# VectorE cuts part of the low halves of the weight panels behind each norm

## The chip, the cores and the metric

The kernel runs on one core of a Trainium2 chip. The metric is device time in microseconds of one execution. The engines are TensorE (PE; its weight loads are shown as PEld), VectorE (DVE), ScalarE (ACT), GpSimd (POOL) and SyncE (SP), which issues the loads of weights.

## What is computed

The reference takes 512 tokens of width 1024 through two blocks of layers, all in float32. Ten stages follow one another. Each ends in a layer norm:

```python
x = layer_norm(DEEPNORM_ALPHA * x + mix, g, b)
# stages: even mixer, cross attention to a memory, swiglu, odd mixer, cross attention, swiglu,
#         hgrn2 + forgetting attention, swiglu, rg_lru + stick-breaking attention, swiglu
def memory_cross_attention(x, mem, wq, wkv, wo):   # mem: 256 tokens
    q = x @ wq;  k, v = split(mem @ wkv)
    return softmax(q k^T) v @ wo
```

Most of the work is products of the 512 (or, for the memory, 256) tokens with weights of width 1024 or 2816.

## The kernel before, in words

**Products.** Float32 values are split in two: a high part, rounded to the type that TensorE multiplies (float32r), and a low part, the difference. `product` (lines 482 to 486) makes each product of three matmuls: high by high, high by low, low by high. So each weight has to be there as a high and a low part.

**Panels.** The weights come in 230 panels of 1 MB (128 partitions by 2048 columns), in the order in which TensorE uses them. Three buffers hold raw panels (`raw`), three hold high parts (`whi`); the low part `wlo` overwrites the raw panel in place. SyncE issues panel n when TensorE is done with panel n-3. The high part is a copy into float32r, in two halves of 1024 columns, by GpSimd (line 2353) or, for the panels in `cut_panels`, by ScalarE (`act_cut`, line 613). The low part is raw minus high, on GpSimd in four quarters of 512 columns (line 2361), one panel after the other. The one exception is the very first panel: VectorE makes its second half (line 2399). TensorE waits in `next_panel` (line 477) for the count of panels that GpSimd has finished:

```python
                for q in range(4 if n else 2):
                    cs = slice(512 * q, 512 * q + 512)
                    ...
                    m = pool.tensor_tensor(wlo[b][:, cs], raw[b][:, cs], whi[b][:, cs].bitcast(F32), ALU.subtract)
                m.then_inc(panel_split, 1)
```

**The end of a stage.** `pe_block_out` multiplies by the down projection (4 or 11 panels). The last three panels are used tile by tile of 128 tokens, so that tiles 0 and 1 are finished early. `dve_block_out` normalises each tile on VectorE: `centre` (lines 721 to 726) adds the product to x and takes off the mean, ScalarE takes the deviation (lines 689, 692), `finish` (lines 732, 733) writes the normalised row. The order on VectorE is centre 0 and 1, finish 0 and 1, the low parts of the turned tiles 0 and 1 (`dve_turn`, line 593), centre 2 and 3, finish 2 and 3. TensorE turns the tiles (`pe_turn`, line 573): tiles 0 and 1 between the last products, tiles 2 and 3 inside the head of the next stage.

**The head of the next stage.** Behind seven of the nine inner norms the next stage uses its first two panels on half of the tokens first (`pe_split`), needing only tiles 0 and 1; tiles 2 and 3 are turned in the middle of the second panel. Behind the other two (before the cross attention stages) come eight panels of `mem_wkv`, called M1 to M8 below, which need no tokens of x: M1 to M3, the turns of tiles 2 and 3, then M4 to M8, and then four panels of the query projection. M1 to M4 use 256-column products, M5 to M8 half as many of 512 columns. Of the panels behind a norm, counted from its last one, ScalarE makes the high parts of 1 and 2 and, before cross attention, of 5 to 8 too.

**Norm rows.** At the start of each stage ScalarE's queue issues two loads (`ln_gb`), 0.5 MB each, which spread the norm's gain and bias over the partitions.

Of the kernel before, what the change touches and what calls it, by code (L numbers as in the profile page):

```python
# [39 lines left out]
NB = 3  # L40
# [13 lines left out]
def build(nc, a, out, stages):  # L54
    with ExitStack() as ctx:
# [220 lines left out]
        panel_hi = sem("panel_hi")  # L276
        panel_hi_act = sem("panel_hi_act")
        panel_split = sem("panel_split")
        first_lo = sem("first_lo")
        panel_used = sem("panel_used")  # L280
        phase = {e: sem(f"phase_{e}") for e in ("pe", "act", "dve")}
        par_loaded = sem("par_loaded")
# [190 lines left out]
        def next_panel(pe, n=1):  # L473

            first = used[0]
            used[0] += n
            pe.wait_ge(panel_split, used[0])
            if first == 0:
                pe.wait_ge(first_lo, 1)
            return [(whi[k % NB], wlo[k % NB]) for k in range(first, first + n)]  # L480

        def product(pe, o, lhs, rhs, start, stop):
# [102 lines left out]
        def dve_turn(dve, dst_hi, dst_lo, k0, blocks, bank, t, gain=None):  # L585
# [3 lines left out]
            for b in range(0, blocks, 4):  # L589
# [4 lines left out]
                else:  # L594
# [9 lines left out]
                               for k in ((0, 1, 2, 5, 6, 7, 8) if program[i + 1:] and program[i + 1][0][0] == "cross"  # L604
                                         else (0, 1, 2)) if n + k < len(panels)]

        def act_cut(act, n):
            assert n in cut_panels
            b = n % NB
            act.wait_ge(panel_loaded[b], 16 * (n // NB + 1))  # L610
            for q in range(2):
                cs = slice(1024 * q, 1024 * q + 1024)
                act.activation(whi[b][:, cs], raw[b][:, cs], ACT.Copy).then_inc(panel_hi_act, 1)  # L613
# [95 lines left out]
        def dve_block_out(dve, step, head, ln_loaded):  # L709
            base = n_ln["dve"]  # L710
            n_ln["dve"] += NT
            dve.wait_ge(*ln_loaded)

            def two_banks(t):
                return PS[:, 2 * t:2 * t + 2, :].rearrange("p a b -> p (a b)")

            def centre(t):

                xt = x_row[:, t, :]
                dve.wait_ge(y_ready, base + t + 1)  # L720
                step(dve.scalar_tensor_tensor(out=xt, in0=xt, scalar=ALPHA, in1=two_banks(t), op0=ALU.mult, op1=ALU.add,  # L721
                                              accum_out=zsum[:, t:t + 1]))
                dve.tensor_scalar(nmean[:, t:t + 1], zsum[:, t:t + 1], -1.0 / D, None, ALU.mult).then_inc(mean_ready, 1)
                dve.wait_ge(mean_ready, base + t + 1)

                step(dve.scalar_tensor_tensor(out=two_banks(t), in0=xt, scalar=nmean[:, t:t + 1], in1=ln_gb[:, 0, :],
                                              op0=ALU.add, op1=ALU.mult))

            def finish(t):

                dve.wait_ge(std_ready, base + t + 1)
                step(dve.reciprocal(rstd[:, t:t + 1], std[:, t:t + 1]))
                dve.scalar_tensor_tensor(out=x_row[:, t, :], in0=two_banks(t), scalar=rstd[:, t:t + 1], in1=ln_gb[:, 1, :],
                                         op0=ALU.mult, op1=ALU.add).then_inc(row_ready, 1)

            centre(0)
            centre(1)
            finish(0)
            finish(1)
            if head:  # L740
                dve_turn(dve, xT_hi, xT_lo, 0, KD, 0, 0)
                dve_turn(dve, xT_hi, xT_lo, 0, KD, 2, 1)
            centre(2)
            if not head:
                finish(2)
            centre(3)
            if head:
                finish(2)
            finish(3)
            if head:  # L750
                head(dve, lambda: (dve_turn(dve, xT_hi, xT_lo, 0, KD, 4, 2), dve_turn(dve, xT_hi, xT_lo, 0, KD, 6, 3)))
# [150 lines left out]
        def stage_cross(st, jobs):  # L902
# [51 lines left out]
            def act(act, step):  # L954
# [11 lines left out]
                act_units(act, A, lambda u: softmax_exp(act, A, u, PS[:, A.ps(u), 0:MEM], 1.0, MEM, A.p(u)))  # L966
                act_rows(act, 0, KD)

            def dve(dve, step):

                def stat(u):
                    dve.wait_ge(s_ready, A.u0 + u + 1)
# [12 lines left out]
            def pe(pe):  # L985
# [15 lines left out]
                def values(u, k):  # L1001
# [3 lines left out]
                pe_rows(pe, c_row, KD, lambda t: A.g0 + 2 * t + 2)  # L1005
            return {"act_load": act_load, "act": act, "dve": dve, "pe": pe,
                    "memory": {"pe": memory_pe, "act": memory_act, "dve": memory_dve},
                    "head": {"pe": head_pe, "act": head_act, "dve": lambda dve, turns: turns()}}

        def stage_ffn(st, jobs):  # L1010
            n0 = counts.get("ffn_tiles", 0)
# [1331 lines left out]
        def _(pool):  # L2343
            shares = {pool_at[i]: c["pool"] for i, c in enumerate(code) if "pool" in c}
            for n in range(len(panels)):
# [6 lines left out]
                    cs = slice(1024 * q, 1024 * q + 1024)  # L2352
                    pool.tensor_scalar(whi[b][:, cs], raw[b][:, cs], 1.0, 1.0, ALU.mult, ALU.mult).then_inc(panel_hi, 1)  # L2353

                for q in range(4 if n else 2):
                    cs = slice(512 * q, 512 * q + 512)
                    if q % 2 == 0 and by_act:
                        pool.wait_ge(panel_hi_act, 2 * cut_panels.index(n) + q // 2 + 1)
                    elif q % 2 == 0:
                        pool.wait_ge(panel_hi, 2 * (n - sum(k < n for k in cut_panels)) + q // 2 + 1)  # L2360
                    m = pool.tensor_tensor(wlo[b][:, cs], raw[b][:, cs], whi[b][:, cs].bitcast(F32), ALU.subtract)  # L2361
# [30 lines left out]
        def _(dve):  # L2392
# [2 lines left out]
            dve.memset(one_col[:, :], 1.0)  # L2395
            dve.wait_ge(par_loaded, 16)
            dve_turn(dve, xT_hi, xT_lo, 0, KD, 0, 0)
            dve.wait_ge(panel_hi_act, 2)
            dve.tensor_tensor(wlo[0][:, 1024:2048], raw[0][:, 1024:2048], whi[0][:, 1024:2048].bitcast(F32), ALU.subtract)\
                .then_inc(first_lo, 1)  # L2400
            dve_turn(dve, xT_hi, xT_lo, 0, KD, 2, 1)
            code[0]["head"]["dve"](dve, lambda: [dve_turn(dve, xT_hi, xT_lo, 0, KD, 2 * t, t) for t in (2, 3)])
            for i, c in enumerate(code):
                c["dve"](dve, step)
                nxt = code[i + 1] if i + 1 < len(code) else None
                if nxt and "memory" in nxt:
# [146 lines left out]
```

## Time and profile before

| what | value |
|---|---|
| median of 3 runs | 3006.47 us (3005.61 to 3013.05) |
| the profiled execution | 3002.93 us |
| its span, first to last instruction | 3001.1 us |
| mean granted clock of TensorE | 0.992 of full speed |
| GpSimd, low parts of panels (line 2361) | 918 quarters, mean 1337 ns |
| GpSimd, high parts (line 2353) | 384 halves, mean 1105 ns |
| ScalarE, high parts (line 613) | 76 halves, mean 1054 ns |
| a panel's load, issue to landing, median | 5.0 to 5.2 us |

A row of the page's groups names the line, the engine, the operation, its output and inputs, the shape, the count, then busy time in us and the mean of one in ns, and last the idle time of the engine before it with what ended it. In a timeline a row is start, duration, engine, line, operation, tiles, shape and count, and in brackets the idle time before. In the chain of waits a row is start, duration and what ran. Durations on GpSimd are rough, so spacings from start to start are used where they are there.

### The profile page before, as it was taken

How to read it: one execution, taken by the hardware profiler on the slowest of the kernel's cores; microseconds unless marked ns; L12 is line 12 of the kernel's file. 1: busy time of each engine (PE TensorE's matmuls, PEld its weight loads, DVE VectorE, ACT ScalarE, POOL GpSimd, SP SyncE). 2: the span in 40 equal slices, each digit the busy share in tenths (PEclk: the TensorE clock that was granted, in tenths of full speed). 3: DMA queues.
4: the chain of work that ended last, by engine and by line, in shares of the span. 5: the costliest groups of instructions: out<-in, count | busy, mean ns of one | idle time of the engine just before them, and what ended most of it. 6: DMA issues, size and time to landing. Idle time of an engine off the chain costs nothing.

```text
span 3001.1 us, 35505 instructions
## 1 busy us (share of the span) xinstructions
PE 2917.3 (97%) x14824; PEld 2436.3 (81%) x14824; DVE 915.2 (30%) x1424; ACT 745.8 (25%) x1492; POOL 1670.7 (56%) x1375
## 2 busy tenths in 40 slices
PE   8989999999999999999999999999999999999998
PEld 7877878888888768788888888788888887888887
DVE  3755204111025482041110334732110238521102
ACT  2236323101024363231110221542000233411001
POOL 5830572666656505726666567526666566066663
PEclk9999999999999999999999999999999998999999
DMA  4231331233223204213222332013222231032222
GB/s 143 95 136 48 125 114 56 99 99 99 98 85 119 71 15 139 99 57 106 93 97 98 103 102 88 11 37 110 94 97 99 98 106 57 31 111 98 98 98 84
DMA packets 184548, 271.21 MB, mean 90 GB/s; under 512 B 6708, under 2 KB 145972, under 8 KB 184388
## 3 DMA queue, kind: packets, MB, share of 16 engines
q1 hardware_dynamic: 174240, 243.28, 24.5%
q10 hardware_dynamic: 10148, 25.66, 2.5%
q8 instruction: 117, 1.92, 0.3%
q14 instruction: 43, 0.35, 0.0%
HBM read 266.79 MB, written 2.13 MB: 90 GB/s over the span
## 4 chain that ended last, share of the span: by engine, by line
PE 80%; DVE 8%; POOL 5%; DMA 4%; ACT 2%; issue 1%; ACTq 0%; DVEq 0%; POOLq 0%
PE PS L484 23%; PE PS L486 23%; PE PS L485 23%; POOL wlo L2361 4%; PE PS L852 3%; PE PS L573 2%; DVE a_qk L1269 1%; PE PS L838 1%; DVE nmx L1604 1%; PE PS L997 1%; DMA raw<-mem_wkv 1%; ACT whi L613 1%; PE PS L1455 1%; DMA raw<-ffn_w 1%; DVE s_c L2249 0%
## 5 line engine op out<-in xcount | busy, mean ns | idle before, releaser
L2361 POOL TENSOR_TENSOR wlo<-raw,whi 128x512 fp32r<-128x512 f32 x918 | 1197.4, 1337 | 538.0 <-ACT whi L613 538.0
L484 PE MATMUL PS<-xT_hi,whi 128*128 128x512 f32 (+1 forms) x2304 | 847.2, 368 | 18.0 <-POOL wlo L2361 9.4
L485 PE MATMUL PS<-xT_lo,whi 128*128 128x512 f32 (+1 forms) x2304 | 842.8, 366 | 0.0
L486 PE MATMUL PS<-xT_hi,wlo 128*128 128x512 f32 (+1 forms) x2304 | 842.7, 366 | 0.0
L2353 POOL TENSOR_SCALAR whi<-raw 128x1024 fp32r<-128x1024 f32 x384 | 417.1, 1105 | 657.4 <-DMA raw<-ffn_w 225.6
L484 PEld LDWEIGHTS PS<-xT_hi,whi 128*128 128x128 f32 x2304 | 435.3, 189 | 93.5 <-POOL wlo L2361 9.9
L485 PEld LDWEIGHTS PS<-xT_lo,whi 128*128 128x128 f32 x2304 | 435.3, 189 | 70.8 <-issue 1.0
L486 PEld LDWEIGHTS PS<-xT_hi,wlo 128*128 128x128 f32 x2304 | 435.3, 189 | 69.7
L1039 DVE TENSOR_TENSOR htmp<-sil,PS 128x512 f32<-128x512 f32 x88 | 56.5, 684 | 804.2 <-ACT sil L1024 804.2
L484 PE MATMUL PS<-whi,h_hi 128*128 128x512 f32 x704 | 274.8, 390 | 1.2 <-POOL wlo L2361 1.2
L486 PE MATMUL PS<-whi,h_lo 128*128 128x512 f32 x704 | 274.0, 389 | 0.0
L485 PE MATMUL PS<-wlo,h_hi 128*128 128x512 f32 x704 | 273.9, 389 | 0.0
L484 PE MATMUL PS<-whi,xT_hi 128*128 128x512 f32 x672 | 264.0, 393 | 4.2 <-POOL wlo L2361 2.1
L486 PE MATMUL PS<-whi,xT_lo 128*128 128x512 f32 x672 | 261.7, 389 | 0.0
L485 PE MATMUL PS<-wlo,xT_hi 128*128 128x512 f32 x672 | 261.6, 389 | 0.0
L1024 ACT ACTIVATE sil<-PS 128x512 f32<-128x512 f32 x88 | 47.9, 597 | 813.3 <-PE PS L486 813.3
L721 DVE SCALAR_TENSOR_TENSOR x_row<-x_row,PS 128x1024 f32<-128x1024 f32 x40 | 48.8, 1221 | 558.8 <-PE PS L486 558.2
L613 ACT ACTIVATE whi<-raw 128x1024 fp32r<-128x1024 f32 x76 | 76.4, 1054 | 520.7 <-DMA raw<-ffn_w 188.1
L484 PEld LDWEIGHTS PS<-whi,h_hi 128*128 128x128 f32 x704 | 132.1, 188 | 29.7 <-POOL wlo L2361 2.5
L486 PEld LDWEIGHTS PS<-whi,h_lo 128*128 128x128 f32 x704 | 132.1, 188 | 27.6
L484 PEld LDWEIGHTS PS<-whi,xT_hi 128*128 128x128 f32 x672 | 126.1, 188 | 34.7 <-POOL wlo L2361 4.6
L485 PEld LDWEIGHTS PS<-wlo,h_hi 128*128 128x128 f32 x704 | 132.2, 188 | 27.1
(384 smaller groups left out, 3107.8 us busy)
## 6 DMA issues: line engine op xcount, KB each, us to landing
raw<-ffn_w SPq DMA_DIRECT2D x66, 1024.0 KB, 5.0
raw<-ffn_w_gu SPq DMA_DIRECT2D x44, 1024.0 KB, 5.1
raw<-ffn_w_down SPq DMA_DIRECT2D x22, 1024.0 KB, 4.9
raw<-mem_wkv SPq DMA_DIRECT2D x16, 1024.0 KB, 5.2
raw<-even_w_in SPq DMA_DIRECT2D x14, 1024.0 KB, 5.2
raw<-ev_w_in SPq DMA_DIRECT2D x14, 1024.0 KB, 5.3
raw<-odd_w_in SPq DMA_DIRECT2D x12, 1024.0 KB, 5.2
raw<-od_w_in SPq DMA_DIRECT2D x10, 1024.0 KB, 5.1
```

The source lines that it names most:

```text
L484: pe.matmul(o, lhs[0], rhs[0], start=start, stop=False, skip_group_check=True)
L485: pe.matmul(o, lhs[0], rhs[1], start=False, stop=False, skip_group_check=True)
L486: return pe.matmul(o, lhs[1], rhs[0], start=False, stop=stop, skip_group_check=True)
L573: m = pe.transpose(PS[:, bank + b // 4, 128 * (b % 4):128 * (b % 4) + 128], src[:, 128 * b:128 * b + 128], ident)
L613: act.activation(whi[b][:, cs], raw[b][:, cs], ACT.Copy).then_inc(panel_hi_act, 1)
L721: step(dve.scalar_tensor_tensor(out=xt, in0=xt, scalar=ALPHA, in1=two_banks(t), op0=ALU.mult, op1=ALU.add, accum_out=zsum[:, t:t + 1]))
L838: m = pe.transpose(PS[:, A.ptb(u), 128 * k:128 * k + 128], A.p(u)[:, 128 * k:128 * k + 128], ident)
L852: m = pe.matmul(PS[:, A.ob(u), c0:c0 + dv], A.pt(u)[:, 128 * k:128 * k + 128], v, start=k == 0, stop=k == A.nk(u) - 1, skip_group_check=True)
L1024: act.activation(sil[:, i % 2, :], PS[:, 2 * j.slot[0] + c, :], ACT.Silu).then_inc(sil_ready, 1)
L1039: m = dve.tensor_tensor(htmp[:, i % 2, :], sil[:, i % 2, :], PS[:, 2 * j.slot[1] + c, :], ALU.mult)
L2353: pool.tensor_scalar(whi[b][:, cs], raw[b][:, cs], 1.0, 1.0, ALU.mult, ALU.mult).then_inc(panel_hi, 1)
L2361: m = pool.tensor_tensor(wlo[b][:, cs], raw[b][:, cs], whi[b][:, cs].bitcast(F32), ALU.subtract)
```

## The change

VectorE makes the last quarter of the low part of the second panel behind each inner norm, and the last half of that of the other memory panels, M1 and M3 to M8 (M2 is a second panel, so a quarter). GpSimd makes what is left of these panels. One subtraction of 512 or 1024 columns per panel replaces one or two quarters: 7 quarter cuts at ordinary norms, 2 quarter cuts and 14 half cuts in the two memory stretches. On VectorE the cut of panel 1 stands behind the low parts of turned tiles 0 and 1, that of panel 2 behind `centre(3)`, those of panels 3 to 5 ahead of turned tiles 2 and 3, and those of 6 to 8 at the start of the cross attention stage. `next_panel` waits for two counts, GpSimd's and VectorE's. The cut of the very first panel is the same as before, issued through the new function.

```diff
--- before.py
+++ after.py
@@ -276,7 +276,7 @@
         panel_hi = sem("panel_hi")
         panel_hi_act = sem("panel_hi_act")
         panel_split = sem("panel_split")
-        first_lo = sem("first_lo")
+        panel_lo_dve = sem("panel_lo_dve")
         panel_used = sem("panel_used")
         phase = {e: sem(f"phase_{e}") for e in ("pe", "act", "dve")}
         par_loaded = sem("par_loaded")
@@ -475,8 +475,9 @@
             first = used[0]
             used[0] += n
             pe.wait_ge(panel_split, used[0])
-            if first == 0:
-                pe.wait_ge(first_lo, 1)
+            shared = sum(k < used[0] for k in dve_cuts)
+            if shared:
+                pe.wait_ge(panel_lo_dve, shared)
             return [(whi[k % NB], wlo[k % NB]) for k in range(first, first + n)]
 
         def product(pe, o, lhs, rhs, start, stop):
@@ -604,6 +605,26 @@
                                for k in ((0, 1, 2, 5, 6, 7, 8) if program[i + 1:] and program[i + 1][0][0] == "cross"
                                          else (0, 1, 2)) if n + k < len(panels)]
 
+
+
+        dve_cuts = {0: (2, 3)}
+        for i, n in enumerate(last_panel[:-1]):
+            memory = program[i + 1][0][0] == "cross"
+            for k in ((1, 2, 3, 4, 5, 6, 7, 8) if memory else (2,)):
+                dve_cuts[n + k] = (3,) if k == 2 else (2, 3)
+        cut_order = sorted(dve_cuts)
+
+        def dve_cut(dve, n):
+            b = n % NB
+            quarters = dve_cuts[n]
+            if n in cut_panels:
+                dve.wait_ge(panel_hi_act, 2 * cut_panels.index(n) + 2)
+            else:
+                dve.wait_ge(panel_hi, 2 * (n + 1 - sum(k < n for k in cut_panels)))
+            cs = slice(512 * quarters[0], 2048)
+            dve.tensor_tensor(wlo[b][:, cs], raw[b][:, cs], whi[b][:, cs].bitcast(F32), ALU.subtract)\
+                .then_inc(panel_lo_dve, 1)
+
         def act_cut(act, n):
             assert n in cut_panels
             b = n % NB
@@ -709,6 +730,7 @@
         def dve_block_out(dve, step, head, ln_loaded):
             base = n_ln["dve"]
             n_ln["dve"] += NT
+            last = last_panel[at_stage[0]]
             dve.wait_ge(*ln_loaded)
 
             def two_banks(t):
@@ -740,11 +762,14 @@
             if head:
                 dve_turn(dve, xT_hi, xT_lo, 0, KD, 0, 0)
                 dve_turn(dve, xT_hi, xT_lo, 0, KD, 2, 1)
+                if last + 1 in dve_cuts:
+                    dve_cut(dve, last + 1)
             centre(2)
             if not head:
                 finish(2)
             centre(3)
             if head:
+                dve_cut(dve, last + 2)
                 finish(2)
             finish(3)
             if head:
@@ -966,7 +991,16 @@
                 act_units(act, A, lambda u: softmax_exp(act, A, u, PS[:, A.ps(u), 0:MEM], 1.0, MEM, A.p(u)))
                 act_rows(act, 0, KD)
 
+            def head_dve(dve, turns):
+                last = last_panel[at_stage[0]]
+                for k in (3, 4, 5):
+                    dve_cut(dve, last + k)
+                turns()
+
             def dve(dve, step):
+                last = last_panel[at_stage[0] - 1]
+                for k in (6, 7, 8):
+                    dve_cut(dve, last + k)
 
                 def stat(u):
                     dve.wait_ge(s_ready, A.u0 + u + 1)
@@ -1005,7 +1039,7 @@
                 pe_rows(pe, c_row, KD, lambda t: A.g0 + 2 * t + 2)
             return {"act_load": act_load, "act": act, "dve": dve, "pe": pe,
                     "memory": {"pe": memory_pe, "act": memory_act, "dve": memory_dve},
-                    "head": {"pe": head_pe, "act": head_act, "dve": lambda dve, turns: turns()}}
+                    "head": {"pe": head_pe, "act": head_act, "dve": head_dve}}
 
         def stage_ffn(st, jobs):
             n0 = counts.get("ffn_tiles", 0)
@@ -2352,7 +2386,7 @@
                     cs = slice(1024 * q, 1024 * q + 1024)
                     pool.tensor_scalar(whi[b][:, cs], raw[b][:, cs], 1.0, 1.0, ALU.mult, ALU.mult).then_inc(panel_hi, 1)
 
-                for q in range(4 if n else 2):
+                for q in range(4 - len(dve_cuts.get(n, ()))):
                     cs = slice(512 * q, 512 * q + 512)
                     if q % 2 == 0 and by_act:
                         pool.wait_ge(panel_hi_act, 2 * cut_panels.index(n) + q // 2 + 1)
@@ -2395,12 +2429,11 @@
             dve.memset(one_col[:, :], 1.0)
             dve.wait_ge(par_loaded, 16)
             dve_turn(dve, xT_hi, xT_lo, 0, KD, 0, 0)
-            dve.wait_ge(panel_hi_act, 2)
-            dve.tensor_tensor(wlo[0][:, 1024:2048], raw[0][:, 1024:2048], whi[0][:, 1024:2048].bitcast(F32), ALU.subtract)\
-                .then_inc(first_lo, 1)
+            dve_cut(dve, 0)
             dve_turn(dve, xT_hi, xT_lo, 0, KD, 2, 1)
             code[0]["head"]["dve"](dve, lambda: [dve_turn(dve, xT_hi, xT_lo, 0, KD, 2 * t, t) for t in (2, 3)])
             for i, c in enumerate(code):
+                at_stage[0] = i
                 c["dve"](dve, step)
                 nxt = code[i + 1] if i + 1 < len(code) else None
                 if nxt and "memory" in nxt:
```

## Rows read from the trace of the kernel before

**Rows 1.** The page's first part, busy time of each engine

```profile
PE 2917.3 (97%) x14824; PEld 2436.3 (81%) x14824; DVE 915.2 (30%) x1424; ACT 745.8 (25%) x1492; POOL 1670.7 (56%) x1375
```

**Rows 2.** The waits of TensorE: line, releaser, us in total, times, longest

```profile
PE PS L484 <- POOL wlo L2361: 23.9, 23, 3.1
```

**Rows 3.** The page's groups by line and shape, half-token products

```profile
L484 PE MATMUL PS<-xT_hi,whi 128*128 128x256 f32 x512 | 148.0, 289 | 15.1 <-POOL wlo L2361 8.5 <-DVE xT_lo L593 6.4
```

**Rows 4.** TensorE's timeline (start, us), first and last of the seven norms

```profile
527.52 0.39 PE L484 MATMUL PS<-xT_hi,whi 128*128 128x256 f32 x1 [1.03 <-POOL wlo L2361]
...
2636.60 0.39 PE L484 MATMUL PS<-xT_hi,whi 128*128 128x256 f32 x1 [1.20 <-POOL wlo L2361]
```

**Rows 5.** TensorE's waits in 325 to 400 and in 1150 to 1220

```profile
PE PS L484 <- POOL wlo L2361: 5.5, 3, 2.9
...
PE PS L484 <- POOL wlo L2361: 6.6, 4, 3.1
```

**Rows 6.** The chain from 512 to 535 (start, us, what), an ordinary norm

```profile
521.44 6.04 POOL wlo L2361 x4
```

**Rows 7.** The chain from 328 to 400, memory stretch one

```profile
349.25 2.03 POOL whi L2353 x2
351.28 4.99 POOL wlo L2361 x4
...
369.91 7.44 DMA raw<-mem_wkv
```

**Rows 8.** Timeline of GpSimd and of VectorE near 15

```profile
14.43 1.27 POOL L2361 TENSOR_TENSOR wlo<-raw,whi 128x512 fp32r<-128x512 f32 x1 [14.00 <-ACT whi L613]
...
15.26 1.52 DVE L2399 TENSOR_TENSOR wlo<-raw,whi 128x1024 fp32r<-128x1024 f32 x1 [0.50 <-ACT whi L613]
...
15.66 2.25 POOL L2361 TENSOR_TENSOR wlo<-raw,whi 128x512 fp32r<-128x512 f32 x1
```

**Rows 9.** Line 726 alone: ns least, median, most

```profile
L726 DVE SCALAR_TENSOR_TENSOR PS<-x_row,nmean,ln_gb x40: 1294/1294/2440, 322.6 to 2994.9; 128x1024 f32<-128x1024 f32 x40
```

**Rows 10.** VectorE's timeline near 523

```profile
522.66 2.44 DVE L726 SCALAR_TENSOR_TENSOR PS<-x_row,nmean,ln_gb 128x1024 f32<-128x1024 f32 x1
```

**Rows 11.** The groups by line and shape, VectorE's 512-column subtraction

```profile
L593 DVE TENSOR_TENSOR xT_lo<-PS,xT_hi 128x512 fp32r<-128x512 f32 x116 | 72.6, 684 | 138.4 <-ACT xT_hi L581 138.4
```

**Rows 12.** VectorE's timeline near 527, last step of the norm

```profile
526.72 1.29 DVE L733 SCALAR_TENSOR_TENSOR x_row<-PS,rstd,ln_gb 128x1024 f32<-128x1024 f32 x1
```

**Rows 13.** TensorE's timeline near 531, turns of tiles 2 and 3

```profile
530.50 1.91 PE L573 MATMUL PS<-par,x_row 128*128 128x128 f32 x16
```

**Rows 14.** TensorE's timeline at its waits in the two memory stretches

```profile
343.38 0.36 PE L484 MATMUL PS<-memT_hi,whi 128*128 128x256 f32 x1 [1.47 <-POOL wlo L2361]
...
356.41 0.36 PE L484 MATMUL PS<-memT_hi,whi 128*128 128x256 f32 x1 [1.08 <-POOL wlo L2361]
...
383.72 0.67 PE L484 MATMUL PS<-whi,memT_hi 128*128 128x512 f32 x1 [2.93 <-POOL wlo L2361]
...
1204.76 0.47 PE L484 MATMUL PS<-whi,memT_hi 128*128 128x512 f32 x1 [3.12 <-POOL wlo L2361]
...
1216.77 0.47 PE L484 MATMUL PS<-xT_hi,whi 128*128 128x512 f32 x1 [0.88 <-POOL wlo L2361]
```

**Rows 15.** ScalarE's timeline near 342, second memory panel

```profile
341.77 2.00 ACT L613 ACTIVATE whi<-raw 128x1024 fp32r<-128x1024 f32 x2 [3.74 <-DMA raw<-mem_wkv]
```

**Rows 16.** Stretches: length, busy us of PE, PEld, DVE, ACT, POOL, clock, DMA, GB/s

```profile
349.40:355.36 5.96, 5.92 (x48) 5.72 (x48) 0.00 (x0) 0.66 (x3) 5.96 (x6) 1.00 0.56 176
383.72:391.04 7.32, 7.32 (x25) 5.91 (x26) 0.00 (x0) 0.00 (x0) 7.32 (x7) 0.77 0.19 65
391.04:396.48 5.44, 5.44 (x25) 4.50 (x24) 0.00 (x0) 0.00 (x0) 4.88 (x5) 1.00 0.61 193
```

**Rows 17.** GpSimd's timeline from 1197 to 1211, memory stretch two

```profile
1199.63 9.98 POOL L2361 TENSOR_TENSOR wlo<-raw,whi 128x512 fp32r<-128x512 f32 x8 [4.97 <-ACT whi L613]
```

**Rows 18.** Line 477 alone, its semaphore instructions: ns least, median, most

```profile
L477 PEldq EVENT_SEMAPHORE  x86: 51/51/5384, 57.3 to 2847.8; - x86
```


## Prediction

> **What bounds the kernel now.** I read the page's first part first. TensorE is busy for 2917.3 of the 3001.1 us span, VectorE for 915.2 and GpSimd for 1670.7 [rows 1]. So only the gaps of TensorE can be won, and the list of TensorE's waits says who ends them: the low parts of weight panels that GpSimd writes (line 2361), 23 times, 23.9 us in all, the longest item there [rows 2]. The change can touch only some of these. The last panel of each down projection stays with GpSimd alone.
>
> The 23.9 us split into three kinds. At the seven norms that no memory stage follows, TensorE waits once for the second panel behind the norm. The grouped line of the half-token products (128x256) gives 8.5 us for these seven, 1.03 at the first of them and 1.20 at the last [rows 3, 4]; none is shorter than the first. In the two stretches with memory panels it is 5.5 us in 3 waits and 6.6 us in 4 [rows 5]. That leaves 3.3 us, the last panels and the like, which stay.
>
> The chain of waits at an ordinary norm shows what stands ahead of the product: behind the panel's load and ScalarE's half of its high part, four quarters on GpSimd, 6.04 us [rows 6]. Four quarters take 4.99 us elsewhere (1.25 each) [rows 7]. The extra 1.0 us comes from VectorE's line 726, and how it comes about decides this case.
>
> **What one moved piece costs.** In the trace VectorE and GpSimd do not read two SBUF inputs side by side. VectorE's existing half cut of the first panel was issued at 15.26, while a GpSimd quarter issued at 14.43 ran, and took 1.52 us. The GpSimd quarter issued at 15.66 took 2.25 us in place of 1.27 [rows 8]. The same happens at norms: the 1024-column operation of line 726 takes 1.29 us in the median and up to 2.44 [rows 9, 10]. So the two engines take turns. VectorE waits for the one quarter that runs, then goes first, and the next quarter waits about 1.0 us.
>
> The Trainium skill, "SBUF — State Buffer", section "Who interferes with whom", states this as a rule: a Vector instruction with two SBUF inputs and a GpSimd instruction that reads SBUF exclude each other. It speaks against the change, and by that rule, the trace agrees, a moved quarter is not free; without it the sum would be that of the first rival below.
>
> So a half cut on VectorE costs the pair 1.0 us and takes away two quarters, 2.5 us: 1.5 us won. For a quarter cut (512 columns) no row exists. It lies between 0, were it hidden, and 0.69, the full length of a 512-column subtraction [rows 11]. I take half of the 1.0, 0.5, as nearest in kind: 0.75 won. For the half cut the ends are 0.98 (2.25 less 1.27) and 1.52.
>
> **Seven ordinary norms.** VectorE gets the quarter cut after it centres the fourth token tile. In five of the seven, line 726 was let in before the second quarter, so after the change the cut goes in before the third, and GpSimd ends 0.75 earlier. In the other two (one is shown: line 726 from 522.66 to 525.10 [rows 10]) the cut is asked for while the third quarter runs, and comes last: GpSimd is done a quarter earlier than the chain's 521.44 + 6.04 = 527.48, at 526.25, and the cut about 0.65 later, at 526.9. That wins 0.6. Each wait is at least 1.03, so it absorbs this: 5 x 0.75 + 2 x 0.6 = 4.9 us. Ends: 7 x 0.5 = 3.5 and, were the cut free, min(wait, 1.25) at each, about 8.2.
>
> Behind the cut on VectorE stand the last two normalisations (lines 732, 733), and TensorE's turns of tiles 2 and 3 wait for them. They now end at 528.01 [rows 12] and would end near 529.8. TensorE comes to those turns near 529.9 (530.50 less 0.6 [rows 13]); its sixteen transposes take 1.91 us there, so the last tile's begin about 0.9 later. That is cover of about 1 us, so cost 0. Without cover each further us costs one us at each norm.
>
> **Memory stretch one** (eight panels, M1 to M8; the waits of TensorE in both stretches stand in [rows 14]).
> - M1: the wait before its first product, 1.47 us, goes: two quarters less and one turn more bring its low part 1.5 us forward.
> - M2: ScalarE begins its high part at 341.77 and ends the first half near 342.85 [rows 15], and GpSimd is free then. Three quarters, line 726 (1.0) and the quarter cut (0.5) are 5.25 us: 348.25, and TensorE starts 0.15 later, at 348.4 in place of 349.4.
> - M3: GpSimd makes its high part (2.03) and two quarters, with one cut between: 353.75. TensorE ends M2 at 348.4 + 5.96 [rows 16] = 354.35, so M3 starts then and not at 356.41: 2.05 us won so far, this wait gone too.
> - M4 to M6 are ready in time now and then. M7's load is issued when M4 is used. It took 7.44 us [rows 7], beside the two loads of the norm's rows from ScalarE's queue, which move along with it. So M7's load starts 2.05 earlier and its low part needs 1.5 less: TensorE starts at 380.15 in place of 383.72, 3.55 won, and a wait of 1.4 us stays there.
> - The products on M7 took 7.32 us at a mean clock of 0.77 against 5.44 on M8 at 1.00 [rows 16]: the clock fell to 1.2 GHz right behind the 2.93 us gap. With the gap halved I count on the 2.4 GHz level: 1.87 us.
> - The first query panel stays whole on GpSimd (7.05 us). Its buffer is free when M6 is used (near 378.75), it lands about 5 us later, and GpSimd is done with it at 390.85. TensorE wants it at 380.15 + 2 x 5.44 = 391.05. It is just covered.
> Sum 5.4 us; without the clock 3.55.
>
> **Memory stretch two.** M1 had no wait. M2 starts 0.7 earlier, M3 1.75 (both waits gone). GpSimd began M7 at 1199.63 after 4.97 us idle [rows 17], so it begins 1.75 earlier and needs 1.5 less: 3.25. The 0.88 us wait of the query panel goes. Sum 4.1 us; here the clock was full behind a gap of 3.12 us, as the products there show (0.47 us for the first against 0.67 in stretch one), so nothing is to be had from it.
>
> **The added waits on TensorE.** Each of the 230 panels now brings a second semaphore. Where a second one stands today it is an instruction of its own in the weight-load queue, 51 ns in the median, 86 of them [rows 18], and such an instruction can pass while the products queued ahead of it run. Cost 0; the upper end, were all exposed, is 229 x 0.051 = 11.7 us. The DMA queue of SP gets no new instruction; ScalarE's order is untouched.
>
> **Sum.** 4.9 + 5.4 + 4.1 = 14.4 us, 0.48%. The span of 3001.1 would be 2986.7, and the profiled execution, 3002.93, stands 3.5 below the median of 3006.47. The same difference from the median gives 2992.
>
> **Rivals.**
> - *No exclusion.* VectorE's cuts run beside GpSimd's. Each norm wins up to its wait, 8.2 in all; with 2.5 in place of 1.5 per memory panel I get 6.1 and 5.9. Together 20.2: 2986. Against it stand both places where the engines took turns [rows 8, 10]. 4%.
> - *VectorE loses the turn.* The cut gets in one GpSimd operation later, behind the next panel's high part. Then each ordinary norm has three quarters, 1.02 and 0.65 against four quarters, a loss of 0.4 and 3 in all, and the memory stretches keep about 6. Net 3: 3003, no change. The turns taken at 15.26 and 522.66 speak against it [rows 8, 10], but neither shows a quarter cut. 8%.
> - *The terms hold in kind but each at its low end:* 3.5 + 3.55 + 3.2, no clock, and timed runs a little off the profile: 9 us or less, 2998. 13%.
> - *VectorE is starved and the norm's tail is late.* GpSimd has no pause behind the third quarter (high part and low part of the third panel, 7 us). Were VectorE let in only then, TensorE would wait 7 us longer at each of seven norms: +49, less the memory gain, about 3045. It decides by how much later than I reckon the cut is let in: at 0.7 us a norm's gain is gone, at 2.1 the seven norms have eaten the 9.5 us of the memory stretches too, at 3.4 the kernel is 9 us slower. The longest delay of line 726 is 1.15 us [rows 9]. 4%.
> The forecast has 71%, its own range 2989 to 2996.
>
> About 0.3% (9 us) is what a measurement of this kernel can tell from no change. So faster by more: 0.75 (forecast and no exclusion); within: 0.21; slower: 0.04. Range 2985 to 3000: it takes in no exclusion and the low ends.
>
> **What would show it.** Right: TensorE's waits on GpSimd fall from 23 to about 20 and from 23.9 us to about 11.5, with the seven at 0.3 to 0.7 each; quarters beside a half cut take near 2.25 us; cuts on VectorE take 1.1 to 2.4; the gap before M7 is 1.4 and the clock in it is full. The time comes out of 500 to 2660 by some 9 us and of 325 to 400 by some 5. Wrong: quarters of 1.25 us beside a cut (no exclusion), a new wait of TensorE on VectorE's low part or on rows of the norm at line 573, or a fall of the clock behind another gap.

## The result, and the profile after

The changed kernel takes 2989.97 us in the median of 6 runs (2986.56 to 3001.97), the kernel before, run beside it, 3007.61 (3005.61 to 3013.05): a ratio of 0.9943, 95% interval 0.9924 to 0.9961. The profiled execution took 2989.39 us with a span of 2987.6, 13.5 less than before; the forecast was 14.4 less.

The first part of the page of after, against [rows 1]: GpSimd has 37 instructions less and is busy 28 us less, VectorE has 23 more and is busy 46 us more.

```profile
PE 2913.4 (98%) x14824; PEld 2434.3 (81%) x14824; DVE 961.7 (32%) x1447; ACT 744.5 (25%) x1492; POOL 1642.4 (55%) x1338
```

TensorE's waits of after (line, releaser, us in total, times, longest), against [rows 2]: 23.9 us in 23 waits have become 9.1 in 21, one of them now on VectorE's own piece. One wait is missing from this list: the 0.79 us before M7, which the profile puts down to "issue"; with it the sum is 9.9, against the 11.5 that were forecast.

```profile
PE PS L485 <- POOL wlo L2395: 8.6, 20, 1.0
...
PE PS L485 <- DVE wlo L625: 0.5, 1, 0.5
```

The group of half-token products, against [rows 3]: the seven norms' waits on a low part fell from 8.5 to 3.5 us (3.0 and 0.5); the 6.4 us behind `xT_lo` are as before.

```profile
L485 PE MATMUL PS<-xT_hi,whi 128*128 128x256 f32 x512 | 148.2, 289 | 10.2 <-DVE xT_lo L594 6.4 <-POOL wlo L2395 3.0 <-DVE wlo L625 0.5
```

TensorE's timeline of after at the first and the last of these norms, against [rows 4], and at its waits in the two stretches, against [rows 14].

```profile
524.68 0.36 PE L485 MATMUL PS<-xT_hi,whi 128*128 128x256 f32 x1 [0.55 <-DVE wlo L625]
...
2623.06 0.39 PE L485 MATMUL PS<-xT_hi,whi 128*128 128x256 f32 x1 [0.47 <-POOL wlo L2395]
...
351.20 0.38 PE L485 MATMUL PS<-memT_hi,whi 128*128 128x256 f32 x1 [0.62 <-POOL wlo L2395]
...
382.17 0.47 PE L485 MATMUL PS<-whi,memT_hi 128*128 128x512 f32 x1 [0.79 <-issue]
393.78 0.47 PE L485 MATMUL PS<-xT_hi,whi 128*128 128x512 f32 x1 [0.45 <-POOL wlo L2395]
```

In stretch one the waits of 1.47, 1.08 and 2.93 us have become one of 0.62 before M2 and one of 0.79 before M7; the one of 0.45 before the first query panel is new. The first product on M7 takes 0.47 us, not 0.67: no fall of the clock behind the smaller gap.

What the chip did with a cut shows in the timelines of VectorE and GpSimd (start, us). First the quarter cut at the norm near 522, then a half cut, of M3.

```profile
520.56 2.28 DVE L748 SCALAR_TENSOR_TENSOR PS<-x_row,nmean,ln_gb 128x1024 f32<-128x1024 f32 x1
522.87 1.66 DVE L625 TENSOR_TENSOR wlo<-raw,whi 128x512 fp32r<-128x512 f32 x1
...
521.71 2.28 POOL L2395 TENSOR_TENSOR wlo<-raw,whi 128x512 fp32r<-128x512 f32 x1
523.96 1.48 POOL L2387 TENSOR_SCALAR whi<-raw 128x1024 fp32r<-128x1024 f32 x1
...
353.22 2.31 DVE L625 TENSOR_TENSOR wlo<-raw,whi 128x1024 fp32r<-128x1024 f32 x1 [0.42 <-POOL whi L2387]
...
353.14 3.54 POOL L2395 TENSOR_TENSOR wlo<-raw,whi 128x512 fp32r<-128x512 f32 x2
```

At 522.87 the cut was issued while GpSimd's third quarter ran. It waited until that ended (523.99), read for about half a microsecond, and the next operation of GpSimd took 1.48 us in place of 1.05. At 353.22 the two quarters beside the half cut took 3.54 us, where two undisturbed ones take 2.55.

Where the time went, when the starts of TensorE's products are compared one by one: the seven norms gave 5.0 us, stretch one 5.3, stretch two 5.2. Ahead of 318 the profiled run of after was 2.9 us late. The loss begins in the first mixer, with a wait of 3.06 us on `a_o` against 0.34 before. Behind it the granted clock is 0.58 in the mean from 142 to 146, where the kernel before has 1.00, and this costs another 1.5 us; near 230 after wins 2.2 back, because there the clock of before is at 0.59 from 227 to 235 and that of after is full. The wait goes back to a small VectorE instruction, `a_row<-g_rows`, which in this one execution took 5.55 us, as long as GpSimd's four quarters beside it:

```profile
54.04 5.55 DVE L1278 TENSOR_SCALAR a_row<-g_rows 4x1024 f32<-4x1024 f32 x1 [18.61 <-ACT g_rows L1133]
...
54.00 5.05 POOL L2395 TENSOR_TENSOR wlo<-raw,whi 128x512 fp32r<-128x512 f32 x4
```

The same instruction before:

```profile
53.50 0.70 DVE L1244 TENSOR_SCALAR a_row<-g_rows 4x1024 f32<-4x1024 f32 x1 [18.64 <-ACT g_rows L1099]
```

### The profile page after: what moved, and what is told of

Same layout as the page of the kernel before. It is cut to its first block, busy times and chain, and to the rows that moved or that the text cites. A ratio compares the mean times of both kernels' runs of the same rounds, so it can differ in the third digit from the quotient of the medians.

```text
span 2987.6 us, 35633 instructions
## 1 busy us (share of the span) xinstructions
PE 2913.4 (98%) x14824; PEld 2434.3 (81%) x14824; DVE 961.7 (32%) x1447; ACT 744.5 (25%) x1492; POOL 1642.4 (55%) x1338
## 3 DMA queue, kind: packets, MB, share of 16 engines
q8 instruction: 117, 1.92, 0.3%
## 4 chain that ended last, share of the span: by engine, by line
PE 81%; DVE 8%; DMA 4%; POOL 3%; ACT 2%; issue 1%; ACTq 0%; DVEq 0%; POOLq 0%
PE PS L485 24%; PE PS L486 23%; PE PS L487 23%; POOL wlo L2395 3%; PE PS L877 3%; PE PS L574 2%; DVE a_qk L1303 2%; PE PS L863 1%; DVE nmx L1638 1%; PE PS L1031 1%; ACT whi L634 1%; DMA raw<-mem_wkv 1%; PE PS L1489 1%; DMA raw<-ffn_w 1%; DVE s_c L2283 0%
## 5 line engine op out<-in xcount | busy, mean ns | idle before, releaser
L2395 POOL TENSOR_TENSOR wlo<-raw,whi 128x512 fp32r<-128x512 f32 x881 | 1169.8, 1360 | 543.4 <-ACT whi L634 543.4
```

## The experiments

Two theories stood. **Taking turns:** VectorE waits for the one GpSimd operation that runs, then reads, and GpSimd's next one waits; each place pays from its own waits, and the parts add up. **Something else**: the gain comes from one part only, the added waits cost, or the cuts delay the norm.

**The change again**, without an edit.

> The changed kernel once more, for a second profile of it. Theory (the engines take turns): TensorE's waits on GpSimd are those of the first profile within 0.2 us each, near 8.6 us in all, and half cuts take 1.5 or 2.3 us. The first profile also lost 3.3 us before 320 us, in the even mixer, where one tensor_scalar of VectorE (the one behind the gates' evacuation) took 5.55 us in place of 0.70. If that belongs to the change, it comes again in this profile; if it is an accident of how the engines' starts fall, it takes 0.7 to 5.6 us here, and the profile of the kernel before could show it as well. Time: 0.993 to 0.996 of before.

It took 2989.23 us (2987.66 to 2995.42), ratio 0.9942 (0.9922 to 0.9962). The waits on low parts were 9.7 us in 19, 1.1 more than expected, and three more stand under "issue": 0.59 and 0.30 us before M7, and 1.92 us before the first panel behind the norm near 515. That last one is new, and the half cuts below show what it is. `a_row<-g_rows` took 1.91 us. So the 5.55 us are no fixed cost of the change; I come back to them at the end.

**The memory panels alone.**

```diff
-            for k in ((1, 2, 3, 4, 5, 6, 7, 8) if memory else (2,)):
+            for k in ((1, 2, 3, 4, 5, 6, 7, 8) if memory else ()):
...
-                dve_cut(dve, last + 2)
+                if last + 2 in dve_cuts:
+                    dve_cut(dve, last + 2)
```

> The cuts of the two memory stretches alone (M1 to M8); at the seven ordinary norms GpSimd makes all four quarters again. Theory: the seven waits are 8.5 us again, those of the stretches stay near 1.3 and 1.7, and the kernel is 9.5 to 10.5 us faster than before, ratio near 0.9967. If the gain came mostly from the norms, it would be about 5 us or less.

2995.37 us (2992.77 to 3009.97), ratio 0.9971 (0.9955 to 0.9987); against the median of before, 3006.03, 10.7 us. The group of half-token products shows six of the seven norms' waits where they were (7.5 us, the 8.5 of [rows 3] less the first norm's 1.03). At the first norm the second panel has no wait, but the first panel has one of 1.8, under "issue", as in the repetition. The waits before M1 to M4 of the two stretches are down to 1.3, from 5.2 (1.47 and 1.08 in stretch one [rows 14], 1.49 and 1.11 in stretch two):

```profile
L485 PE MATMUL PS<-xT_hi,whi 128*128 128x256 f32 x512 | 148.5, 290 | 15.9 <-POOL wlo L2396 7.5 <-DVE xT_lo L594 6.4 <-issue 1.8
...
L485 PE MATMUL PS<-memT_hi,whi 128*128 128x256 f32 x128 | 36.6, 286 | 1.3 <-POOL wlo L2396 1.3
```

**The ordinary norms alone.**

```diff
-            for k in ((1, 2, 3, 4, 5, 6, 7, 8) if memory else (2,)):
+            for k in (() if memory else (2,)):
...
-                dve_cut(dve, last + 2)
+                if last + 2 in dve_cuts:
+                    dve_cut(dve, last + 2)
...
-                for k in (3, 4, 5):
-                    dve_cut(dve, last + k)
```

(and the same for 6 to 8.)

> The quarter cuts at the seven ordinary norms alone; M1 to M8 are GpSimd's alone. Theory: 4.9 us faster than before, ratio near 0.9984, the seven waits 0.3 to 0.7 us each, the stretches 5.5 and 6.6 as before. Rival (the tail of the norm comes late): the waits at the norms do not fall or TensorE waits at line 573.

2998.1 us (2994.91 to 3012.34), ratio 0.9975 (0.9961 to 0.999): 7.9 us by the medians, an interval that holds the 4.9. The norms' waits are those of the change, in the page's group:

```profile
L485 PE MATMUL PS<-xT_hi,whi 128*128 128x256 f32 x512 | 148.4, 290 | 10.2 <-DVE xT_lo L594 6.5 <-POOL wlo L2392 3.5
```

and TensorE's timeline has the gap before M7 back:

```profile
397.83 0.47 PE L485 MATMUL PS<-whi,memT_hi 128*128 128x512 f32 x1 [3.14 <-ACT c_v L968]
```

The gaps of the two stretches are 6.4 and 5.5 us in this profile, where 5.5 and 6.6 were expected: the sum is right, its parts shift. So within the noise the parts add up: by the medians they give 10.7 and 7.9, together 18.6, against 16.8 for both, and each removes the waits at its own places and not the other's. The product behind the 3.14 us gap took 0.47 us: here the clock did not fall.

The profiled execution of this kernel took 3012.34 us, 14 above its own median. TensorE's windows say why (window, us, busy and instructions, granted clock, DMA share, GB/s): 112 matmuls in 28 us at clock 0.50,

```profile
226.00:234.00 8.00, 6.29 (x20) 0.69 0.07 29
234.00:262.00 28.00, 28.00 (x112) 0.50 0.11 38
```

where the change's run does 60 to 62 in 8 us at full clock:

```profile
238.00:246.00 8.00, 8.00 (x62) 1.00 0.11 20
246.00:254.00 8.00, 8.00 (x60) 1.00 0.28 113
```

**The added waits alone**: the kernel before, whose every panel now also waits for the count of the first panel's second half, long since reached.

```diff
-            if first == 0:
-                pe.wait_ge(first_lo, 1)
+            pe.wait_ge(first_lo, 1)
```

> The kernel before with one edit: TensorE waits for first_lo, long since reached, at every panel and not at the first alone. No cut is moved. Theory: the added waits cost nothing, 0 to 1 us. Rival: they are exposed, 51 ns each at 229 panels, 11.7 us, ratio 1.004; then the moves themselves are worth more than the change shows.

3003.25 us (3000.19 to 3015.59), ratio 0.9988 (0.9973 to 1.0003). The group of these instructions in the weight-load queue (ns least, median, most) has become 219 large, and they cost nothing that can be measured; the 11.7 us of full exposure are excluded.

```profile
L478 PEldq EVENT_SEMAPHORE  x219: 51/51/7111, 16.9 to 2976.2; - x110
```

**The cut behind the norm's last tile.** This moves one line, and tests what the place of the cut is worth.

```diff
                 if head:
-                    dve_cut(dve, last + 2)
                     finish(2)
                 finish(3)
+                if head:
+                    dve_cut(dve, last + 2)
```

> The change with the quarter cut of the second panel behind finish(3) and not ahead of finish(2). Theory: the cut is asked for 2.9 us later, when GpSimd is in the third panel's high part, and each of the seven waits becomes 2.3 to 2.9 us, 17 to 20 us in all in place of 3.6; 14 to 17 us slower than the change, about as the kernel before. It shows the decision point of the starved rival: every us by which the cut comes later costs one us at each norm. If the cut's place did not matter, the time stays at that of the change.

2999.13 us (2996.03 to 3007.84), ratio 0.9984 (0.9973 to 0.9994): 4.8 us faster than the kernel before beside it (3003.91), where the change's repetition was 16.8 faster. So most of the gain is gone, 12 us, a little less than the 14 to 17 expected. The waits have changed their owner, 15.6 us in 9 (12.1 of them at the seven norms; less than I expected, because the cut met the end of GpSimd's high part and had to wait less than half a microsecond, 0.68 to 1.14 us long in all):

```profile
PE PS L485 <- DVE wlo L625: 15.6, 9, 2.5
...
PE PS L485 <- POOL wlo L2395: 4.9, 10, 0.8
```

VectorE's timeline at one norm shows the cut, here 0.88 us long, in the queue behind the two rows of `finish`, and (last row, TensorE's own timeline) the product starting 0.14 us after it:

```profile
520.35 1.28 DVE L755 SCALAR_TENSOR_TENSOR x_row<-PS,rstd,ln_gb 128x1024 f32<-128x1024 f32 x1
...
521.74 1.28 DVE L755 SCALAR_TENSOR_TENSOR x_row<-PS,rstd,ln_gb 128x1024 f32<-128x1024 f32 x1
522.94 0.88 DVE L625 TENSOR_TENSOR wlo<-raw,whi 128x512 fp32r<-128x512 f32 x1
...
523.96 0.35 PE L485 MATMUL PS<-xT_hi,whi 128*128 128x256 f32 x1 [2.46 <-DVE wlo L625]
```

**Larger cuts.** If a quarter cut costs half a microsecond and a half cut one, a half at the second panel should win 1.5 us where the quarter wins 0.75, and most of the norms' waits should go.

```diff
-                dve_cuts[n + k] = (3,) if k == 2 else (2, 3)
+                dve_cuts[n + k] = (2, 3)
```

> The change with a half cut on VectorE, and two quarters on GpSimd, for the second panel too (seven norms, and M2). Theory: GpSimd ends 0.5 to 0.6 us earlier once more there (1.0 added by the turn for the half, less 0.44 for the quarter, against 1.25 saved), the seven waits fall from 3.6 us to under 1, and the norm's last rows come 0.5 later, which the cover of about 1 us hides. 3 us faster than the change, ratio near 0.993. Rival: the cover is gone and TensorE waits at line 574 for tile 3, as long as it gained.

2985.83 us (2979.35 to 2993.37), ratio 0.9941 (0.9928 to 0.9954), waits on low parts 5.1 us. In six of the seven norms at most 0.2 us is left: the waits went as expected, but the ratio cannot be told from the change's 0.9943. At the seventh norm 1.45 us stand before the first panel, put down to "issue". The timelines of GpSimd, VectorE and TensorE show that it is a wait on a low part too:

```profile
519.24 2.26 POOL L2395 TENSOR_TENSOR wlo<-raw,whi 128x512 fp32r<-128x512 f32 x1
...
518.91 1.45 DVE L748 SCALAR_TENSOR_TENSOR PS<-x_row,nmean,ln_gb 128x1024 f32<-128x1024 f32 x1
...
521.59 0.36 PE L485 MATMUL PS<-xT_hi,whi 128*128 128x256 f32 x1 [1.45 <-issue]
```

The fourth quarter of the first panel took 2.26 us, because the last step of `centre` (line 748) was let in ahead of it, and TensorE starts 0.09 us after its end. In the change's first profile that step came while the fourth quarter ran, and delayed nothing there. ScalarE's high part began 6.8 us after the issue of the panel's load here, and 6.0 us after it there; why the load took longer is open. The 1.92 us of the repetition and the 1.8 of the memory panels alone have the same fourth quarter, 2.27 and 2.26 us. This panel was left to GpSimd by every version. Then also three quarters of the other memory panels:

```diff
-                dve_cuts[n + k] = (2, 3)
+                dve_cuts[n + k] = (2, 3) if k == 2 else (1, 2, 3)
```

> As half_at_norms, and three quarters on VectorE for M1 and M3 to M8: GpSimd makes one quarter (1.25), VectorE 1536 columns (about 1.55). Theory: 0.7 us less per panel, so the wait before M7 (0.3 to 1.0 us in each stretch) and that of the query panel go; 1 to 2 us faster than half_at_norms. Rival: M7's load, not the cut, ends this wait, and nothing changes.

2983.69 us (2980.51 to 2989.07), ratio 0.9934 (0.9921 to 0.9947), 2 us by the medians and again less than the intervals can tell; waits on low parts 5.6 us: none at the seven norms, but 0.78 and 1.49 at the query panels and 0.2 to 0.5 at the last panels. So those were cut as well:

```diff
-            for k in ((1, 2, 3, 4, 5, 6, 7, 8) if memory else (2,)):
-                dve_cuts[n + k] = (2, 3) if k == 2 else (1, 2, 3)
+            for k in ((1, 2, 3, 4, 5, 6, 7, 8, 9) if memory else (2,)):
+                dve_cuts[n + k] = (2, 3) if k in (2, 9) else (1, 2, 3)
+        for n in last_panel:
+            dve_cuts[n] = (2, 3)
```

(with the cut of the last panel ahead of `centre(0)`, and that of the query panel behind those of 6 to 8.)

> Three quarters of the memory panels, halves of the second panels, and now also half of the last panel of each down projection (ahead of centre(0)) and half of the first query panel. Theory (what is left is the slack of GpSimd at each place, and a larger cut buys it as long as VectorE is idle there): the waits left in three_quarters at the last panels and the query panels (0.78 and 1.49 us for the queries, 0.2 to 0.5 at several norms, 5.7 us in all) fall under 2 us in all, and the kernel is 3 to 5 us faster than three_quarters, ratio to before 0.991 to 0.993. Rival (VectorE's cut ahead of the centring delays the norm's own statistics by what it takes, 1.5 us, and the norm is the path): the waits in front of the attention or gate work behind the norm grow by as much, and the kernel is level with three_quarters or up to 5 us slower (ratio 0.993 to 0.996).

2978.58 us (2977.26 to 2987.07), before beside it 3009.88, ratio 0.9901 (0.9885 to 0.9917). This version beats the kernel before and, with intervals that just don't meet, the change; against the version before it, it is 5.1 us faster by the medians, where 3 to 5 were forecast. All that TensorE still waits for low parts is

```profile
PE PS L485 <- DVE wlo L627: 1.2, 3, 0.7
```

and none of it is GpSimd's. The rival, that a cut ahead of the centring delays the norm, fell: no other wait of TensorE grew by more than 0.2 us against the three quarters, and the time fell.

**A probe behind the cut: do one-input instructions take turns too?** The single 5.55 us instruction has one input. So the change got one more VectorE instruction right behind the second panel's cut, on a row of `ln_gb` that is not read again in that stage.

```diff
                 dve_cut(dve, last + 2)
+                step(dve.tensor_scalar(ln_gb[:, 0, 0:512], ln_gb[:, 0, 0:512], 1.0, None, ALU.mult))
```

> The change with one operation more behind the second panel's cut, at all nine norms: a tensor_scalar of VectorE over 512 columns in place in the norm's gain row, which is no longer read. It has one SBUF input and an SBUF output, like the one that took 5.55 us in the first profile of the change. GpSimd has six or more operations in a row there. Theory A (operations of this kind are not let in between GpSimd's and wait for a pause of it): it takes 4 to 7 us, the norm's last rows come that much later, TensorE waits 3 to 6 us at line 574 at each norm, and the kernel is 25 to 45 us slower than the change. Theory B (the 5.55 us had another cause, this kind takes turns too): 0.3 to 1.6 us, and at most 5 us slower.

The second probe, in its place, multiplies the gain row by the bias row:

```diff
+                step(dve.tensor_tensor(ln_gb[:, 0, 0:512], ln_gb[:, 0, 0:512], ln_gb[:, 1, 0:512], ALU.mult))
```

> The change, with a VectorE instruction of two inputs (128x512, in place of the one-input probe) behind the cut of the second panel at nine norms. If both kinds take turns alike with GpSimd: the next GpSimd quarter is lengthened by roughly what the probe's own data phase takes, as behind the cuts (0.4 us), against 0.1 to 0.2 us behind the one-input probe; waits of TensorE on the second panel stay near 3 us over the seven norms.

The group of the one-input probe, then of the two-input one (ns least, median, most):

```profile
L773 DVE TENSOR_SCALAR ln_gb<-ln_gb x9: 414/1499/1508, 345.9 to 2620.3; 128x512 f32<-128x512 f32 x9
```

```profile
L773 DVE TENSOR_TENSOR ln_gb<-ln_gb x9: 679/1766/1770, 346.0 to 2625.1; 128x512 f32<-128x512 f32 x9
```

Once in nine, at the norm near 521, GpSimd had nothing running when it was issued: 414 and 679 ns are their own lengths. In the other eight each waited about 1.1 us more, for the one quarter that ran. What GpSimd lost differs. Its next operation, 1.05 us when alone, took 1.18 to 1.23 behind the one-input probe,

```profile
884.56 1.73 POOL L2396 TENSOR_TENSOR wlo<-raw,whi 128x512 fp32r<-128x512 f32 x1
886.30 1.18 POOL L2388 TENSOR_SCALAR whi<-raw 128x1024 fp32r<-128x1024 f32 x1
```

and 1.49 or 1.50 in seven of eight cases behind the other:

```profile
885.10 1.73 POOL L2396 TENSOR_TENSOR wlo<-raw,whi 128x512 fp32r<-128x512 f32 x1
886.79 1.49 POOL L2388 TENSOR_SCALAR whi<-raw 128x1024 fp32r<-128x1024 f32 x1
```

Where cut and probe were queued one behind the other and GpSimd was busy, the engines alternated, one operation each. The Trainium skill, "SBUF — State Buffer", section "Who interferes with whom", says that a `tensor_scalar` in a two-port mode contends with GpSimd too. The trace agrees that this one contends (1.50 us against 0.41); no row shows its mode. The times, 2986.81 (two runs) and 2992.69 (one run), tell nothing against the change's, and no wait of TensorE on rows of the norm came: the cover of the norm's tail holds at least one more such instruction.

**The norm rows' loads moved away from M7's.** In the change as before they are issued from ScalarE's queue when M7's load runs. Here they stand behind the stage's own work on ScalarE; the dots are the two loads.

```diff
+                if c["kind"] == "cross":
+                    c["act"](act, step)
...
-                c["act"](act, step)
+                if c["kind"] != "cross":
+                    c["act"](act, step)
```

> The change, with the loads of the cross norm's rows issued behind the load of the activations, so that they don't run beside the load of the first stretch's seventh memory panel. Theory (that load takes 6.8 to 7.4 us where its neighbours take about 5 because other transfers run beside it): it takes 5 to 5.5 us, the wait of TensorE before that panel (0.3 to 1.0 us in the runs with the change) is gone, 0.3 to 1.0 us in all, which the ratio (0.994) hardly shows. Rival (the load is slow for itself, or the transfers beside it are others): 6.8 us or more again and the wait is there.

2989.68 us (2984.29 to 3003.02), ratio 0.9939 (0.9916 to 0.9963): no difference in time. M7's load, issued at 370.50 in the change, let ScalarE begin at 377.35; the DMA view from 368 to 382 gives the two queues (packets, MB, share of 16 engines)

```profile
q1 hardware_dynamic: 1056, 2.10, 43.8%
q10 hardware_dynamic: 288, 1.05, 27.8%
```

and in ScalarE's timeline the high part of M7 is

```profile
377.35 2.01 ACT L634 ACTIVATE whi<-raw 128x1024 fp32r<-128x1024 f32 x2 [6.18 <-DMA raw<-mem_wkv]
```

With the rows later the load was issued at 366.36 and ScalarE began 4.9 us after it (5.0 in stretch two). In every other profile with M7's load beside the rows' it began 6.0 to 7.8 us after the issue. The timelines of ScalarE and, behind the dots, of TensorE at the query panel:

```profile
371.27 1.06 ACT L634 ACTIVATE whi<-raw 128x1024 fp32r<-128x1024 f32 x1 [4.24 <-DMA raw<-mem_wkv]
...
389.56 0.47 PE L485 MATMUL PS<-xT_hi,whi 128*128 128x512 f32 x1 [1.45 <-POOL wlo L2395]
```

So what the load took beyond 5 us was the other transfers. The wait before M7 is gone, and nothing is won: TensorE waits 1.45 us for the first query panel, whole on GpSimd, in both stretches, in place of 0.45 and 0.19. The chain of waits of the same kernel (start, us, what) is a row of things that none of this shortens:

```profile
377.27 4.92 DMA raw<-mem_wq
382.26 2.07 POOL whi L2387 x2
384.33 4.99 POOL wlo L2395 x4
```

## Why the prediction was right, and where its terms were off

**That the engines take turns, and what a cut costs the pair.** Right. The half cut costs the quarter behind it 0.98 us as at 15.66 [rows 8], and all 24 cuts of after lie between 1.52 and 2.31 us. The quarter cut, for which no row stood, was put at 0.5: the operation behind it is longer by 0.43 to 0.49 (1.48 against 1.05, 1.73 against 1.25). The rival without exclusion would have left the norms with next to no wait; they kept 3.6 us. The rival in which VectorE loses its turn fell with the timeline at 522.87.

**Seven norms, 4.9 us.** Measured 4.93 by the waits, 3.6 us left of 8.5. The norm near 522 went as drawn for "the cut comes last": TensorE starts 0.15 us after VectorE's piece. At the other six (five were forecast) the cut was let in before the third quarter. What the forecast did not have is the first panel behind the norm: in the repetition it cost 1.92 us at one norm.

**The norm's tail, cost 0.** Right: no new wait on line 574, not even with a probe added. That the order on VectorE was the point is shown by the kernel with the cut behind `finish(3)`, which keeps 4.8 us where the change's repetition has 16.8, each against the kernel before beside it.

**Stretch one, 5.4 us.** Measured 5.3, from terms that were each somewhat off, so that the match of the sum is partly luck. Up to M3 2.27 us were won (2.05 forecast). Up to M7 it was 4.5 in place of 3.55: M7's load took 6.83 us, not the 7.44 of [rows 7] that I carried over. The clock gave back 1.5 to 1.6 of the 1.87 us. Against that, "it is just covered" failed: the query panel waited 0.45 us. The margin there was 0.2 us, and TensorE was almost a microsecond earlier than reckoned.

**Stretch two, 4.1 us.** Measured 4.95 by its waits, 5.2 by the starts of the products: the step that failed is M7 again, 3.25 forecast and 4.26 measured by the waits, 0.35 of it from M2 and M3 and the rest from the load, 7.00 us in place of 7.64. The query panel kept 0.19 us.

**The added waits, cost 0.** Right, and shown by themselves.

**The sum.** 15.4 us from the three terms, by the starts of the products, against 14.4; 2.9 were lost before 318, and 1.0 is left of the 13.5. That rest is no single thing: the product starts show 2.0 us won at the late fall of the clock (20.5 us long against 23.9 before), 1.5 lost at a fall near 1818 that before has not (mean clock 0.66 from 1818 to 1823, against 1.00 before), and about 0.5 in small differences. By the medians it was 17.6 and, in the repetition, 16.8 us: the profile of before lay 4.7 us under its median of this comparison, that of after 0.6. The forecast took the 14.4 off the median; 2992 came out 2 us high. So close a match is partly luck: the interval of the ratio spans 12 to 23 us of gain. The range from 2985 to 3000 was set by the low ends and by no exclusion; the runs of one kernel alone spread by 15 us.

## What to carry to other kernels

Two engines that exclude each other can still share a job, when the second is the faster one at it and can wait for its turn: here a quarter costs the pair 0.5 us on VectorE where GpSimd needs 1.25, a half 1.0 against 2.5. Look for all places where the first engine's work ends last, and put the piece ahead of what is needed latest in the second's queue: the same instruction behind the norm's last two rows gave back most of the gain. And when a wait is removed, write down the next thing in the same chain with its margin: the query panel took over what the load of M7 gave free.

## What the runs showed that I had not expected

**A clock that falls for different lengths, and goes with much of the scatter.** In all profiles the granted clock of TensorE falls to 0.50 where TensorE has gaps, mostly in the mixers, for 3.4 to 34.1 us, at the same few places and not in every run. 28 us at 0.50 let 112 matmuls pass where some 210 do at full clock, a loss of about 14 us, and executions of one kernel differ by as much. The four runs with the rows later go from 2984.29 us at a mean clock of 0.994 to 3003.02 at 0.988. The clock is not all of it: two runs of the kernel before took 3003.91 us at 0.990 and 3012.50 at 0.991. Behind a gap of about 3 us before M7 it fell in two of four cases: in stretch one of before (2.93) and of the kernel with the waits alone (2.95), not in stretch two of before (3.12) nor in stretch one with the norms alone (3.14), whose window has the full clock:

```profile
397.00:402.00 5.00, 4.17 (x19) 1.00 0.42 146
```

The 1.87 us that I counted as regained is therefore a gain in some executions only.

**One instruction that waited through four.** `a_row<-g_rows` took 0.70 to 1.91 us in all other profiles and 5.55 once, and every cut and probe was let in after one operation of GpSimd. That exception cost 2.7 us of waiting in one execution, and 1.5 more through the clock behind the wait, and stays unexplained; the probe shows only that a one-input instruction does take turns.
